# A shared expert's products behind the first pass of a mixture of experts: moving matrix products past a ring of weight slots

## The reference, cut to what matters

```python
scores = sigmoid(x @ router_w); ... eidx = top_k(masked sel, 8); w = normalised scores * 2.5
routed = routed_experts(x, eidx, w, wg, wu, wd)          # 64 experts, FF = 256: (silu(x@wg)*(x@wu))@wd, times w
shared = (jax.nn.silu(x @ swg) * (x @ swu)) @ swd        # one expert that every token takes
return routed + shared
```

## Time and profile before

| | us |
|---|---|
| median of three runs | 1458.41 (1456.27 to 1458.91) |
| the profiled execution, its own time | 1459.88 |
| its span, first to last instruction | 1457.7 |
| TensorE busy | 1401.5 (96%) |
| VectorE busy | 437.6 (30%) |
| ScalarE busy | 317.1 (22%) |
| GpSimd busy | 48.1 (3%) |
| mean granted TensorE clock | 0.992 |
| moved by DMA | 509.61 MB, mean 350 GB/s |

### The profile page before, as it was taken

One profiled execution on the slowest core, in us unless ns is written; L12 is line 12 of the kernel. 1 busy time (PEld: TensorE's weight loads), 2 busy tenths in 40 slices (PEclk: granted clock), 3 DMA queues, 4 the chain that ended last, 5 costly groups with the idle time before them and its releaser, 6 DMA issues.

```text
span 1457.7 us, 20775 instructions
## 1 busy us (share of the span) xinstructions
PE 1401.5 (96%) x8288; PEld 708.6 (49%) x8288; DVE 437.6 (30%) x1161; ACT 317.1 (22%) x746; POOL 48.1 (3%) x86
## 2 busy tenths in 40 slices
PE   7999999999999999999799999999999999999977
PEld 3345656444544454444365456564444454445433
DVE  1146435312222222221345243442122212222213
ACT  2135332111111111111345122411111111111112
POOL 0100301000000000000100010010000000000000
PEclk9999999999999999999999999999999999999998
DMA  9999536999999999999953255479999999999991
GB/s 394 377 395 390 205 133 279 383 408 423 408 425 426 424 425 425 426 425 424 369 204 143 116 216 184 142 317 403 406 426 420 422 416 426 425 427 425 424 423 55
DMA packets 48001, 509.61 MB, mean 350 GB/s; under 512 B 5808, under 2 KB 6208, under 8 KB 8320
## 3 DMA queue, kind: packets, MB, share of 16 engines
q1 hardware_dynamic: 26864, 364.19, 60.3%
q10 hardware_dynamic: 17280, 125.84, 20.9%
q0 software_dynamic: 3760, 18.23, 3.4%
HBM read 499.20 MB, written 11.01 MB: 350 GB/s over the span
## 4 chain that ended last, share of the span: by engine, by line
PE 86%; DMA 6%; DVE 3%; ACT 3%; issue 1%; SPq 0%; DVEq 0%; ACTq 0%
PE bank L2022 26%; PE banks L2072 12%; PE banks L1924 9%; DMA s_gu_ring<-in_moe_up_dram 5%; PE banks L445 5%; PE banks L1120 3%; PE ybank L1952 3%; PE banks L1952 3%; PE bank L1954 3%; PE bank L507 2%; PE ybank L1716 1%; PE banks L1716 1%; DMA s_gu_ring<-in_ada_w_dram 1%; PE banks L699 1%; PE banks L1125 1%; PE banks L673 1%
## 5 line engine op out<-in xcount | busy, mean ns | idle before, releaser
L2022 PE MATMUL bank<-s_gu_ring,s_hbuf 128*32 128x512 f32 (+1 forms) x2688 | 399.1, 599 | 18.5 <-DMA s_gu_ring<-in_moe_up_dram 17.6
L2022 PEld LDWEIGHTS bank<-s_gu_ring,s_hbuf 128*32 128x32 f32 (+1 forms) x2688 | 123.0, 120 | 285.9 <-issue 285.9
L2072 PE MATMUL banks<-s_dn_ring,s_hTs 128*32 128x512 f32 (+1 forms) x1344 | 204.2, 596 | 1.7 <-DMA s_dn_ring<-in_moe_wd_dram 1.7
L2198 DVE TENSOR_TENSOR s_ylo<-banks,s_yhi 128x512 fp32r<-128x512 f32 x112 | 77.5, 692 | 322.2 <-ACT s_yhi L2114 322.2
L1924 PE MATMUL banks<-s_sel,s_htok 128*128 128x512 f32 (+1 forms) x640 | 144.8, 374 | 0.5 <-issue 0.5
L1924 PEld LDWEIGHTS banks<-s_sel,s_htok 128*128 128x128 f32 x640 | 106.3, 188 | 60.7 <-issue 44.3
L2114 ACT CAST s_yhi<-banks 128x512 fp32r<-128x512 f32 x112 | 65.7, 586 | 298.4 <-PE banks L2072 298.4
L2193 DVE SCALAR_TENSOR_TENSOR s_hh<-s_sg,s_wsl,bank 128x256 f32<-128x256 f32 x56 | 26.9, 480 | 309.2 <-ACT s_sg L2105 309.2
L2072 PEld LDWEIGHTS banks<-s_dn_ring,s_hTs 128*32 128x32 f32 (+1 forms) x1344 | 56.3, 118 | 119.5 <-issue 118.8
L2105 ACT ACTIVATE s_sg<-bank 128x256 f32<-128x256 f32 x56 | 21.6, 385 | 385.9 <-PE bank L2022 385.9
L2153 DVE COPY s_hbuf<-banks 128x512 f32<-128x512 f32 (+1 forms) x60 | 39.4, 656 | 96.0 <-PE banks L1924 96.0
(11 more groups left out here) (463 smaller groups left out, 1453.7 us busy)
## 6 DMA issues: line engine op xcount, KB each, us to landing
s_gu_ring<-in_moe_up_dram SPq DMA_DIRECT2D x128, 2048.0 KB, 15.0
s_dn_ring<-in_moe_wd_dram ACTq DMA_DIRECT2D x120, 1024.0 KB, 17.5
s_gu_ring<-in_ada_w_dram SPq DMA_DIRECT2D x24, 2048.0 KB, 12.5
s_gu_ring<-in_win_dram SPq DMA_DIRECT2D x6, 2048.0 KB, 15.3
s_dn_ring<-in_moe_wd_dram SPq DMA_DIRECT2D x8, 1024.0 KB, 10.3
s_gu_ring<-in_wqkv_dram SPq DMA_DIRECT2D x6, 1024.0 KB, 19.4
s_gu_ring<-in_wo_dram SPq DMA_DIRECT2D x2, 2048.0 KB, 13.2
s_gu_ring<-in_shared_up_dram SPq DMA_DIRECT2D x2, 2048.0 KB, 12.7
```

The costliest lines, as they stand in the source:

```text
L2022: last = pe.matmul(W0[o:o + n, :], tokens_of(p, k)[:, o:o + n], w[:, k, :, :], start=(k == 0), stop=(k == KC - 1))
L2072: last = pe.matmul((W1, W2)[half][o:o + n, :], hTs[:, f, o:o + n], dn_ring[:, DN_PLACE[dn_of[(l, r)][0]], w0:w0 + 512], start=(f == 0), st ...
L2198: dve.tensor_tensor(ylo[:, half, :], (W1, W2)[half], yhi[:, half, :].bitcast(F32), ALU.subtract).then_inc(S["y_low"], 1)
```

## The change

Of the 16 k-steps of the shared expert's half 1, four (gate, k = 0 to 3) stay before the passes; the other twelve and the drain move behind the gate-and-up product of pass 0, and with them ScalarE's silu and VectorE's product of half 1. Since `hT` is then still read, the first gathers go elsewhere: pass 0's rows into `x0`, which lies where `yhi` is later, pass 1's into the last quarter of `hbuf`, which `hT` does not touch; each copy of a first fill becomes two half copies. Batch 1 is laid into `hbuf` from its front. Load order 4 takes the slot of pass 0's first expert in place of the shared one, order 5 that of the second, order 6 the shared one, and then the order repeats with period five.

```diff
@@ expert_slots(l): which ring slot each expert's up weights take
+            slots = [(units[0] + x) % NGU for x in range(NGU)]
+            units[0] += NE + 1
             for r in LOAD_ORDER[l]:
-                s = units[0] % NGU
-                units[0] += 1
                 i = LOAD_ORDER[l].index(r)
+                s = slots[i] if i < NGU - 1 else slots[(0, 1, 4, 2, 3)[(i - NGU + 1) % NGU]]
                 d = i % DN_EARLY if i < 2 * DN_EARLY else (i + 1) % NDN
@@ moe(l), TensorE before the passes
+                    def shared_up(pe, f, u, ks):
+
+                        for k in ks:
+                            last = pe.matmul(bank[2 + 2 * f + u][:, 0:T], shw[:, k, FF * u + P * f:FF * u + P * f + P], hT[:, k, :],
+                                             start=(k == 0), stop=(k == KC - 1))
+                        return last
...
                         last.then_inc(S["pw_psum"], 1)
-                        shared_up(1, 0, range(KC))
+                        shared_up(pe, 1, 0, (0,))
                         pe.wait_ge(S["pwT_full"], l + 1)
                         for t in range(3):
                             for u in range(2):
                                 last = pe.matmul((W2, W1)[u][:, 64 * t:64 * t + 64], pwT[64 * u:64 * u + 64, t, :],
                                                  perm[64 * u:64 * u + 64, :], start=True, stop=True)
                         last.then_inc(S["sort_psum"], 1)
-                        pe.wait_ge(A["mod_full"], mod_at(19 + 4 * l))
-                        shared_up(1, 1, range(KC)).then_inc(S["sh_psum"], 1)
-                        item_used.up(pe.drain())
+                        shared_up(pe, 1, 0, range(1, 4))
@@ ScalarE before the passes
                         act.copy(wovS[:, :, :], W1[:, 0:192].rearrange("p (t e) -> p t e", t=3)).then_inc(S["w_parts"], 1)
-                        act.wait_ge(S["sh_psum"], 2 * l + 2)
-                        act.activation(ovh[:, 1, :], bank[4][:, 0:T], ACT.Silu).then_inc(S["sh_silu"], 1)
@@ places of the gathered rows
+                with ExitStack() as c3:
+                    x0 = sb("x0", [P, KC, P], c=c3)
                 yhi, ylo = (sb(n, [P, 2, 512], F32R, c=c2) for n in ("yhi", "ylo"))
...
                 xg = hbuf[:, :].rearrange("p (b u s) -> p b u s", b=4, s=P)
+                first_xg = (x0, xg[:, 3, :, :])
...
                     if q == 0:
-                        return xg[:, j, k, :]
+                        return first_xg[j][:, k, :]
                     if q % 2:
-                        return xg[:, (k // 2 + 2 * (q == 1)) % 4, 4 * (k % 2) + j, :]
+                        return xg[:, k // 2, 4 * (k % 2) + j, :]
...
                     if q == 0:
-                        return xg[:, 0:n, 2 * f:2 * f + 2, :]
+                        return [x[:, 2 * f:2 * f + 2, :] for x in first_xg]
                     if q % 2:
-                        return xg[:, (f // 2 + 2 * (q == 1)) % 4, 4 * (f % 2):4 * (f % 2) + n, :]
-                    return xg[:, 0:n, 4 * (f % 2) + f // 2, :]
+                        return [xg[:, f // 2, 4 * (f % 2):4 * (f % 2) + n, :]]
+                    return [xg[:, 0:n, 4 * (f % 2) + f // 2, :]]
@@ TensorE, in the loop over the passes, behind the gate-and-up product
                         last.then_inc(S["gu_full"], 1)
+                        if p == 0:
+                            shared_up(pe, 1, 0, range(4, KC))
+                            pe.wait_ge(A["mod_full"], mod_at(19 + 4 * l))
+                            shared_up(pe, 1, 1, range(KC)).then_inc(S["sh_psum"], 1)
+                            item_used.up(pe.drain())
                         fills = fills_in(p)
@@ ScalarE in the passes (fill_out of VectorE alike, with tensor_copy)
                         act.wait_ge(S["fill_full"], filled(q, f))
-                        act.copy(fill_target(q, f), fill_source(q, f)).then_inc(S["fill_act"], 1)
+                        for dst, src in zip(fill_target(q, f), fill_source(q, f)):
+                            last = act.copy(dst, src)
+                        last.then_inc(S["fill_act"], 1)
...
                         act.activation(sg[:, :], W0[:, 0:FF], ACT.Silu).then_inc(S["silu_full"], 1)
+                        if p == 0:
+                            act.wait_ge(S["sh_psum"], 2 * l + 2)
+                            act.activation(ovh[:, 1, :], bank[4][:, 0:T], ACT.Silu).then_inc(S["sh_silu"], 1)
@@ VectorE
-                    dve.wait_ge(S["sh_silu"], 2 * l + 2)
-                    dve.tensor_tensor(ovh[:, 1, :], ovh[:, 1, :], bank[5][:, 0:T], ALU.mult).then_inc(S["sh_h"], 1)
                     dve.wait_ge(S["h_kept"], 16 * (l + 1))
...
                         dve.scalar_tensor_tensor(hh[:, :], sg[:, :], wsl[p % 2][:, 0:1], W0[:, FF:2 * FF], ALU.mult, ALU.mult).then_inc(S["hh_full"], 1)
+                        if p == 0:
+                            dve.wait_ge(S["sh_silu"], 2 * l + 2)
+                            dve.tensor_tensor(ovh[:, 1, :], ovh[:, 1, :], bank[5][:, 0:T], ALU.mult).then_inc(S["sh_h"], 1)
```

More of the change, by code:

```diff
@@ L1711, in _ @@
                         pe.transpose(W2[:, 64:128], sigT[0:64, 1, :], ident[0:64, 0:64]).then_inc(S["r_psum"], 1)
[L1713 to L1718, removed]
                         slot_in[sg_].wait(pe, sg_n)
-                        shared_up(0, 0, range(2))
+                        shared_up(pe, 0, 0, range(2))
                         for n in range(2, 6):
@@ L1745, in _ @@
                         pe.matmul(W1[:, 128:192], up2[0:NS, :], m2, start=False, stop=True).then_inc(S["cnt_psum"], 1)
-                        shared_up(0, 0, range(6, KC))
-                        shared_up(0, 1, (0,))
+                        shared_up(pe, 0, 0, range(6, KC))
+                        shared_up(pe, 0, 1, (0,))
                         pe.wait_ge(S["perm_full"], l + 1)
@@ L1750, in _ @@
                         pe.matmul(W0[0:1, 448:512], cols[0:NE, 2:3], perm[0:NE, :], start=True, stop=True).then_inc(S["sort_psum"], 1)
-                        shared_up(0, 1, range(1, KC)).then_inc(S["sh_psum"], 1)
+                        shared_up(pe, 0, 1, range(1, KC)).then_inc(S["sh_psum"], 1)
                         pe.wait_ge(S["pw_full"], l + 1)
@@ L1893, in fill_source @@
                     if q == 0:
-                        return b.rearrange("p (m j s) -> p j m s", m=2, s=P)
-                    return b[:, 0:n * P].rearrange("p (j s) -> p j s", s=P)
+                        by_pass = b.rearrange("p (m j s) -> p j m s", m=2, s=P)
+                        return [by_pass[:, j, :, :] for j in range(n)]
+                    return [b[:, 0:n * P].rearrange("p (j s) -> p j s", s=P)]
                 def filled(q, f):
@@ L2152, in fill_out @@
                         dve.wait_ge(S["fill_full"], filled(q, f))
-                        dve.tensor_copy(fill_target(q, f), fill_source(q, f)).then_inc(S["fill_dve"], 1)
+                        for dst, src in zip(fill_target(q, f), fill_source(q, f)):
+                            last = dve.tensor_copy(dst, src)
+                        last.then_inc(S["fill_dve"], 1)
                     dve.wait_ge(S["tok_lo"], 3 * (l + 1))
```

4 lines of the change are left out of this document (2 added, 2 removed).

## The result

The changed kernel took 1461.26 us (median of 8 runs, 1459.92 to 1464.19), the kernel before 1459.04 (8 runs). The medians are 2.2 us apart. The ratio estimated from all runs is 1.0019, with a 95% interval of 1.0010 to 1.0028: about 2.8 us slower (1.5 to 4.1). The forecast was 3.1 us slower.

The account below looks back on a forecast made before the run. TensorE was taken to bound passes 0 to 25 and the weight stream pass 27. Terms -5.56 + 6.75 + 0.26 + 0.12 gave +1.57 us a layer, +3.1 for two: 1461.5 us from 1458.41, range 1457.2 to 1464.2.

Parts of the forecast that it names:

- Case A: Before the first gather: GpSimd's third subtraction holds VectorE's selection; 1461.5 us, own range 1459.5 to 1463; chance 0.5.
- B: Before the first gather: the selection isn't held, so +0.67 us a layer, 1459.7 us, not slower; chance 0.2.
- C: Weight stream alone governs, -0.5 us a layer; clock kept before pass 27, 1.8 more a layer; 1453.8 us; chance 0.08.
- D: First gather's fills two and three wait for half copies; +0.6 us a layer on Case A, 1462.7 us; chance 0.14.
- What bounds, and that the stream gains nothing: TensorE sets passes 0 to 25, the stream pass 27; pass 1's delay goes through whole; new load order gains nothing.
- signs of being wrong: Pass 1 no later, pass 1 waiting for order 4, or the 1.6 us shift kept to pass 26 but not 27.
- Step (a): TensorE in front of the position products: they start near 232.3 us, gap 0 to 0.1.
- Step (b): In front of the first gather: selection held to 236.03 us, gather starts 5.56 us earlier; unheld 6.46 earlier.
- Step (c): First fills, two half copies for one: most covered, the last VectorE copy before pass 0 adds 0.12 to 0.16 us.
- (d): Pass 0's product starts at 242.15 us in place of 247.59 and releases 5.4 us earlier.
- (e): Behind pass 0's product: 24 moved matmuls, 6.75 us, and the drain, 0.26 us (bounds 0 and 0.5).
- Sum: Pass 1's start in one layer: +1.57 us, or +0.67 with nothing held; two layers +3.1 or +1.3.

Follow-up runs that it names:

- the last run: Up half moved, no drain, early word after VectorE's first half copy; added against that kernel: 22 idle TensorE products before pass 27's load wait. 1455.05 us.

## Why the prediction was right, and where it was not

The forecast was +3.1 us (1461.5), in a range of 1457.2 to 1464.2; measured are +2.8 by the ratio, +2.2 by the medians, and 1461.26. The closeness of 1461.26 to 1461.5 is in part luck: the forecast stood on a median before of 1458.41, which is 1459.04 with more runs. Case A has the time, but its mark in the profile did not come; B, C and D did not hold.

- *What bounds, and that the stream gains nothing*: right. Pass 1 did not wait for load order 4, the passes up to 25 kept their shift, and the doubled up half shows that a delay goes through. One of my signs of being wrong, a pass 27 that doesn't keep the shift, did stand in layer 1 of the profiled execution; the repeated runs put it down to scatter. The balance of the first loads, on which I spent most of this step, did not matter: the old ring order started them 6.2 us late and it cost nothing that the runs can see. I had read one lull at 382 us; the slack up to 390 us was some 5.5 us.
- *Step (a), no gap in front of the position products*: right. They began at 232.14, 0.06 us behind the copy of pwT and 0.03 behind the products in front.
- *Step (b), the held selection*: right in its price, wrong in its first cause, and so in part luck. I overlooked that VectorE itself waits for `tok_lo` (L2155 of the kernel before) in front of `select(0)`, a wait that I had listed for TensorE only. My mark for this step was a first L2133 of 1.6 us; it was 0.56, behind 1.49 us of waiting. By my own test (0.56 or about 1.6) that length spoke for rival B, while the time was A's: both locks open at the end of the same subtraction, so even with no holding at all the named wait would have given A's sum. The holding is a second lock behind the first one and nearly as dear: the run without the named wait shows the 1.62 us that I had forecast, and that the two don't add up. The Trainium skill (SBUF — State Buffer, section "Who interferes with whom") has the later of two such instructions block fully; that run agrees, 1.62 against 0.56 us. The gather started 5.23 us earlier, not 5.56: 0.19 of the difference is the named wait, the other 0.14 stands in the run without it as well, half of it in the 0.14 us of issue behind the selection, for which I had put 0.07. No run took both locks away.
- *Step (c), half copies*: the copies were covered, as said, and from the gather's start to pass 0's it took only 0.03 us more, not 0.12. Most likely that is no cheaper copy: ScalarE's copy of the slot weights ended last there both before and after (0.21 us in front of pass 0), and I had not listed that wait.
- *Steps (d) and (e)*: pass 0 began 5.40 us earlier, as said, but 0.20 of that stood in front of the stretch; in it, it is 5.20. The moved matmuls and the drain took 6.79 us more between pass 0 and pass 1, not 7.01. A moved matmul costs 0.27 us (4.3 us for 16 in the run with the up half twice), not 0.281, so 24 cost some 6.5; the drain costs some 0.35, not 0.26. The two errors partly cancel. In the kernel before, the drain cost 0.26 of issue and 0.21 of overlap in front of the gather, and I took the larger part only.
- *Sum*: -5.23 + 6.79 + 0.03 = +1.59 a layer, against -5.56 + 6.75 + 0.26 + 0.12 = +1.57. The sum is closer than its terms, and that is luck: 0.33 too much gain in (b) and 0.31 too much cost in (c) and (e) cancel.
- *Rival C* was right that the clock before pass 27 is worth 1.8 us a layer, as the last run shows, but wrong that this change could win it: the wait stayed at 7.4 and 5.6 us, and pass 27's product took 9.91 and 8.74 us.

What stays open: whether the new ring order would be worth something where TensorE isn't the bound up to pass 25. It wasn't tried. Open as well are the last wait in front of pass 0 and the missing part of the gain in the last run.

## What to carry to other kernels

Work that fills an engine's wait is free where it stands; moved past the wait it costs its own length again, as far as it leaves a gap behind. Before moving it, list every wait between the old place and the new one, on all engines and in the program text, and see what will release each when the cover is gone: here eight k-steps could go and cost nothing, twelve cost 1.6 us a layer, and fifteen cost 4.8 and 5.8 (3.2 with the clock held), since the gap then took the clock down. When two locks hold the same step, take away both before you expect the time back.

## What the runs showed of the hardware that I had not expected

- Behind 3.18 us without work on TensorE the granted clock stood at 1.2 GHz in place of 2.4 for most of the gather (7.67 us in place of 5.07), in layer 1 behind 3.19 us only for a later part of it (6.52 us); behind 1.39 us it stayed at 2.4. With the gap filled by 12 idle products it stayed as well.
- A drain between two groups of products costs some 0.35 us on TensorE, of which only 0.11 stand as issue in the chain. The rest is overlap that is lost: without it the next group starts 0.40 us before the recorded end of the one in front. The chain hides this, since it counts the overlap to the earlier group; the stretch between two fixed starts shows it.
- A VectorE operation that GpSimd holds is recorded with its start at issue and a length that includes the holding (1.62 us); one that waits for a semaphore is recorded with its own length behind idle time (0.56 behind 1.49). The two can be told apart by that.
